# A three-mixer transformer kernel: the triangle inversion starts from a transpose and ends in 64x64 blocks, and the compressed product uses four column groups

## What is computed

```python
def step(state, inp):
    r_t, w_t, k_t, v_t, a_t, b_t = inp
    sa = jnp.einsum('bhvk,bhk->bhv', state, a_t)
    state = (state * w_t[:, :, None, :] + sa[..., None] * b_t[:, :, None, :]
             + v_t[..., None] * k_t[:, :, None, :])
    return state, jnp.einsum('bhvk,bhk->bhv', state, r_t)
```

```python
flat = blocks.transpose(0, 1, 3, 2, 4).reshape(B, nc, G, NSA_CMP_BLOCK * hd)
return jax.nn.gelu(flat @ w1) @ w2
```

## Time and profile before

| | us |
|---|---|
| median of 3 runs | 2197.66 (2193.72 to 2198.87) |
| the profiled execution's own time | 2200.27 |
| its span in the profile | 2198.5 |
| PE busy | 2054.9 (93% of the span) |
| DVE busy, ACT busy | 608.1, 316.1 |
| mean granted TensorE clock | 0.965 of full speed |

### The profile page before, as it was taken

How to read it: one execution, slowest core, us unless ns; L and a number is a source line. 1 busy time by engine, 2 the same in 40 slices (tenths; PEclk the granted TensorE clock), 3 DMA queues, 4 the chain that set the end, 5 groups by cost and what they waited for, 6 DMA issues and landing times.

```text
span 2198.5 us, 24406 instructions
## 1 busy us (share of the span) xinstructions
PE 2054.9 (93%) x9982; PEld 1171.2 (53%) x9982; DVE 608.1 (28%) x1191; ACT 316.1 (14%) x703; POOL 65.0 (3%) x68
## 2 busy tenths in 40 slices
PE   8988999999998999999778999999999999999996
PEld 7766688847766678846634333333333333333332
DVE  0467453312367430004632111111111111111112
ACT  1324110001324210002420000000000000000001
POOL 0022000000022000000010000000000000000000
PEclk9989999999979999999886999999999999999999
DMA  7430078864320045444107999999999999999995
GB/s 296 153 116 1 1 283 303 344 229 171 144 96 31 20 165 228 153 166 153 48 7 290 409 428 429 428 428 429 429 428 428 429 428 429 429 428 427 429 428 252
DMA packets 43823, 599.77 MB, mean 273 GB/s; under 512 B 4992, under 2 KB 5296, under 8 KB 7888
## 3 DMA queue, kind: packets, MB, share of 16 engines
q1 hardware_dynamic: 43760, 598.87, 66.5%
HBM read 597.78 MB, written 1.07 MB: 272 GB/s over the span
## 4 chain that ended last, share of the span: by engine, by line
PE 68%; DMA 22%; DVE 7%; ACT 1%; issue 1%; SPq 0%; DVEq 0%; ACTq 0%
DMA ring<-in_stream 22%; PE ps L1821 14%; PE ps L1234 14%; PE ps L1255 7%; PE ps L376 6%; PE ps L1848 3%; PE ps L390 2%; PE ps L1161 2%; PE ps L1803 2%; PE ps L1898 2%; PE ps L1810 2%; PE ps L1586 1%; PE ps L777 1%; PE ps L789 1%; DVE SB L762 1%
## 5 line engine op out<-in xcount | busy, mean ns | idle before, releaser
L1821 PE MATMUL ps<-ring,HT 128*64 128x512 f32 x2176 | 488.8, 599 | 11.0 <-DMA ring<-in_stream 11.0
L1821 PEld LDWEIGHTS ps<-ring,HT 128*64 128x64 f32 x2176 | 147.9, 137 | 326.5 <-issue 277.1
L1234 PE MATMUL ps<-XT,ring 128*128 128x256 f32 (+1 forms) x1536 | 306.0, 362 | 3.3 <-DVE XT L313 3.3
L1234 PEld LDWEIGHTS ps<-XT,ring 128*128 128x128 f32 x1536 | 271.9, 190 | 36.8 <-DVE XT L313 3.7
L1848 PE MATMUL ps<-ring,HT 128*64 128x512 f32 x1088 | 248.0, 598 | 33.7 <-DMA ring<-in_stream 32.8
L1848 PEld LDWEIGHTS ps<-ring,HT 128*64 128x64 f32 x1088 | 72.6, 136 | 196.1 <-issue 121.3
L1255 PE MATMUL ps<-ring,HT 128*128 128x512 f32 x352 | 151.7, 592 | 0.0
L376 PE MATMUL ps<-XT,ring 128*128 128x256 f32 x576 | 126.6, 383 | 1.3 <-DMA ring<-in_stream 1.3
L1956 DVE TENSOR_SCALAR HT<-ps 128x512 f32<-128x512 f32 x34 | 23.5, 692 | 350.3 <-PE ps L1821 350.3
L376 PEld LDWEIGHTS ps<-XT,ring 128*128 128x128 f32 x576 | 110.7, 192 | 17.0 <-issue 1.7
L1255 PEld LDWEIGHTS ps<-ring,HT 128*128 128x128 f32 x352 | 66.7, 190 | 82.4 <-issue 82.3
(11 more groups left out here) (394 smaller groups left out, 1841.0 us busy)
## 6 DMA issues: line engine op xcount, KB each, us to landing
ring<-in_stream SPq DMA_DIRECT2D x278, 2048.0 KB, 14.6
SB<-in_ln SPq DMA_DIRECT2D x8, 512.0 KB, 9.6
SB<-mod_rows SPq DMA_DIRECT2D x1, 3072.0 KB, 9.8
CST<-in_const SPq DMA_DIRECT2D x1, 1362.0 KB, 5.4
PAR<-in_layer SPq DMA_DIRECT2D x2, 558.5 KB, 11.2
X<-in_x SPq DMA_DIRECT2D x1, 1024.0 KB, 4.9
HN<-in_head_norm SPq DMA_DIRECT2D x2, 512.0 KB, 12.1
SB<-in_gains SPq DMA_DIRECT2D x2, 512.0 KB, 9.8
```

The source lines that it names most:

```text
L1234: m = pe.matmul(ps[:, 2 * (f % 2) + a, j * T + cols.start:j * T + cols.stop], w[:, k, a, j * P:(j + 1) * P], XT[:, k, cols], start=k == 0, ...
L1821: m = pe.matmul(ps[HD * half:HD * (half + 1), a, :], XE[:, 2 * b + k, q * SLOTS_E:(q + 1) * SLOTS_E], w[:, k, a, half, :], start=False, st ...
```

## The change

1. `TM` and `TT` are no longer set to identities. The first level of both halves is done without a product: DVE masks the triangle into `MK` and adds the identity into `TT` (`inverse_first_dve`); PE transposes the eight masked matrices through banks 5 and 6 (`inverse_first_pe`), DVE adds the identity to the transposes and writes `TM` (`inverse_turned_dve`).
2. The last level (half steps 12 and 13) takes only the one 64x64 block per unit that is off the diagonal: four 64x64 products from `MM` itself without a mask, a 64x256 copy on ACT, four 64x64 products for `TT` alone, and one 64x256 copy on DVE in place of two 128x512 adds.
3. The loop starts at half step 2 (h = s+2) and has 18 steps. The attention keeps its lag of two steps, so attention unit u goes with half step u+4, and units 10 and 11 share their steps with the first chunk's parts. The early output projection of t=0 moves from steps 17 and 18 of 20 to steps 16 and 17 of 18.
4. The compressed product's two sums over 16 matmuls become four sums over 8, one in each group of 32 columns of the array (PSUM rows 0 to 127 instead of 0 to 63); the number of matmuls stays 32. DVE adds the two halves (one 64x256 copy more, and an add where a copy was).

```diff
-            L(nc.vector.tensor_copy(SM[:, 32:40], ps[:, 4, 0:8]))
-            v.wait_ge(S("start_loaded"), 32)
-            idb = ident.unsqueeze(1).broadcast_to([P, 8, P])
-            I(nc.vector.tensor_copy(TM, idb))
-            nc.vector.tensor_copy(TT, idb).then_inc(S("rw_init"), 1)
+            nc.vector.tensor_copy(SM[:, 32:40], ps[:, 4, 0:8]).then_inc(S("rw_init"), 1)
...
+        def inverse_done(l, s):
+
+            return 26 * l + (s + 3 if s < 2 else 2 * s + 2 if s < 12 else s + 13)
+
+        def inverse_first_dve(v, l):
+
+            idb = ident.unsqueeze(1).broadcast_to([P, 4, P])
+            v.wait_ge(S("start_loaded"), 32)
+            for s in range(2):
+                us = inverse_half(s)
+                nc.vector.tensor_tensor(MK[:, us, :], MM[:, us, 0, :], inverse_mask(s), ALU.mult).then_inc(S("rw_mk"), 1)
+            for s in range(2):
+                us = inverse_half(s)
+                v.wait_ge(S("rw_mk"), 12 * l + s + 1)
+                nc.vector.tensor_tensor(TT[:, us, :], MK[:, us, :], idb, ALU.add).then_inc(S("rw_tm"), 1)
+
+        def inverse_first_pe(pe, l):
+            pe.wait_ge(S("rw_bk"), l + 1)
+            for s in range(2):
+                pe.wait_ge(S("rw_mk"), 12 * l + s + 1)
+                for i in range(4):
+                    m = pe.transpose(ps[:, 5 + s, i * P:(i + 1) * P], MK[:, 4 * s + i, :], ident)
+                m.then_inc(S("rw_z_ps"), 1)
+
+        def inverse_turned_dve(v, l):
+            idb = ident.unsqueeze(1).broadcast_to([P, 4, P])
+            for s in range(2):
+                v.wait_ge(S("rw_z_ps"), 14 * l + s + 1)
+                nc.vector.tensor_tensor(TM[:, inverse_half(s), :], ps[:, 5 + s, :].rearrange("p (u s) -> p u s", u=4), idb,
+                                        ALU.add).then_inc(S("rw_tm"), 1)
...
+            if s < 4:
+                pool.wait_ge(S("rw_tm"), 26 * l + s - 1)
...
         def inverse_update_dve(v, l, s):
-            us = slice(4 * (s % 2), 4 * (s % 2) + 4)
-            v.wait_ge(S("rw_dt"), 14 * l + s + 1)
-            if s >= 2:
-                v.wait_ge(S("rw_tm"), 28 * l + 2 * s - 2)
+            us = inverse_half(s)
+            v.wait_ge(S("rw_dt"), 12 * l + s - 1)
+            v.wait_ge(S("rw_tm"), inverse_done(l, s - 2))
+            if s >= 12:
+                nc.vector.tensor_copy(TT[0:HD, us, HD:P], ps[0:HD, 7, 0:256].rearrange("p (u s) -> p u s", u=4)
+                                      ).then_inc(S("rw_tm"), 1)
+                return
...
+            pe.wait_ge(S("rw_tm"), inverse_done(l, s - 2))
+            if s > 2:
+                pe.wait_ge(S("rw_zc"), 12 * l + s - 2)
+            if s < 12:
+                pe.wait_ge(S("rw_mk"), 12 * l + s + 1)
             for i in range(4):
                 u = 4 * (s % 2) + i
-                m = pe.matmul(ps[:, 5, i * P:(i + 1) * P], MK[:, u, :], TM[:, u, :], start=True, stop=True)
+                if s < 12:
+                    m = pe.matmul(ps[:, 5, i * P:(i + 1) * P], MK[:, u, :], TM[:, u, :], start=True, stop=True)
+                else:
+                    m = pe.matmul(ps[HD:P, 5, i * HD:(i + 1) * HD], MM[0:HD, u, 0, HD:P], TM[0:HD, u, 0:HD], start=True, stop=True)
...
+            if s == 2:
                 pe.wait_ge(S("cmp_x"), l + 1)
+            if s >= 12:
+                for i in range(4):
+                    u = 4 * (s % 2) + i
+                    m = pe.matmul(ps[0:HD, 7, i * HD:(i + 1) * HD], ZM[HD:P, u, 0:HD], TT[HD:P, u, HD:P], start=True, stop=True)
+                m.then_inc(S("rw_dt"), 1)
+                return
...
-            for j in range(16):
-                for i in range(2):
-                    m = pe.matmul(ps[32 * i:32 * (i + 1), 7, 0:256], N_FL[i][:, j, :], w[i][:, j, :], start=j == 0, stop=j == 15)
+            for j in range(8):
+                for half in range(2):
+                    for i in range(2):
+                        q = 2 * half + i
+                        m = pe.matmul(ps[32 * q:32 * (q + 1), 7, 0:256], N_FL[i][:, 8 * half + j, :], w[i][:, 8 * half + j, :],
+                                      start=j == 0, stop=j == 7, tile_position=(0, 32 * q))
...
-            nc.vector.tensor_copy(x, ps[0:64, 7, 0:256]).then_inc(S("cmp_x"), 1)
+            L(nc.vector.tensor_copy(y, ps[64:128, 7, 0:256]))
+            nc.vector.tensor_tensor(x, y, ps[0:64, 7, 0:256], ALU.add).then_inc(S("cmp_x"), 1)
...
-        HALF_LEVELS, ATT_LAG = 14, 2
-        STEPS = HALF_LEVELS + 6
+        FIRST_HALF, HALF_LEVELS, ATT_LAG = 2, 14, 2
+        STEPS = HALF_LEVELS - FIRST_HALF + 6
...
-            inverse_product_pe(pe, l, 0)
+            inverse_first_pe(pe, l)
+            inverse_product_pe(pe, l, FIRST_HALF)
             for s in range(STEPS):
                 u, at = s - ATT_LAG, NU * l + s - ATT_LAG
-                j, part = divmod(s - HALF_LEVELS, 3)
-                if s + 1 < HALF_LEVELS:
-                    inverse_product_pe(pe, l, s + 1)
+                h = s + FIRST_HALF
+                j, part = divmod(h - HALF_LEVELS, 3)
+                if h + 1 < HALF_LEVELS:
+                    inverse_product_pe(pe, l, h + 1)
                 if unit_scores(u):
                     attention_scores_pe(pe, at)
-                if s < HALF_LEVELS:
-                    inverse_update_pe(pe, l, s)
+                if h < HALF_LEVELS:
+                    inverse_update_pe(pe, l, h)
...
-                if s in (STEPS - 3, STEPS - 2):
-                    mix_early_pe(pe, l, 0, s - (STEPS - 3))
+                if s in (STEPS - 2, STEPS - 1):
+                    mix_early_pe(pe, l, 0, s - (STEPS - 2))
...
-            inverse_level_dve(v, l, 0)
-            inverse_level_dve(v, l, 1)
+            inverse_first_dve(v, l)
             gla_mask_dve(v, l)
+            inverse_turned_dve(v, l)
             cmp_hidden_dve(v, l, L)
```

More of the change, by code:

```diff
@@ L739, in rwkv_mask_dve, with inverse_half, inverse_mask @@
                                     ALU.mult).then_inc(S("rw_mm"), 1)
-        def inverse_level_dve(v, l, s):
-            n, us = s // 2, slice(4 * (s % 2), 4 * (s % 2) + 4)
-            lev = cst("levels")[:, n * P:(n + 1) * P].unsqueeze(1).broadcast_to([P, 4, P])
-            nc.vector.tensor_tensor(MK[:, us, :], MM[:, us, 0, :], lev, ALU.mult).then_inc(S("rw_mk"), 1)
+        def inverse_half(s):
+            return slice(4 * (s % 2), 4 * (s % 2) + 4)
+        def inverse_mask(s):
+            return cst("levels")[:, (s // 2) * P:(s // 2 + 1) * P].unsqueeze(1).broadcast_to([P, 4, P])
@@ L756, in inverse_update_dve @@
+            nc.gpsimd.tensor_tensor(MK[:, us, :], MM[:, us, 0, :], inverse_mask(s), ALU.mult).then_inc(S("rw_mk"), 1)
         def inverse_update_dve(v, l, s):
-            us = slice(4 * (s % 2), 4 * (s % 2) + 4)
-            v.wait_ge(S("rw_dt"), 14 * l + s + 1)
-            if s >= 2:
-                v.wait_ge(S("rw_tm"), 28 * l + 2 * s - 2)
+            us = inverse_half(s)
+            v.wait_ge(S("rw_dt"), 12 * l + s - 1)
[4 more added lines that the diff above has]
+                return
@@ L796, in inverse_product_act @@
             act.wait_ge(S("rw_z_ps"), 14 * l + s + 1)
-            if s >= 2:
-                act.wait_ge(S("rw_dt"), 14 * l + s - 1)
-            g = 4 * (s % 2)
-            nc.scalar.activation(ZM[:, g:g + 4, :].rearrange("p u s -> p (u s)"), ps[:, 5, :], ACT.Copy).then_inc(S("rw_zc"), 1)
+            if s >= 4:
+                act.wait_ge(S("rw_dt"), 12 * l + s - 3)
+            us = inverse_half(s)
+            if s < 12:
+                to, src = ZM[:, us, :].rearrange("p u s -> p (u s)"), ps[:, 5, :]
+            else:
+                to, src = ZM[HD:P, us, 0:HD], ps[HD:P, 5, 0:256].rearrange("p (u s) -> p u s", u=4)
+            nc.scalar.activation(to, src, ACT.Copy).then_inc(S("rw_zc"), 1)
         def chunk_removed_pe(pe, l, j):
             if j == 0:
-                pe.wait_ge(S("rw_tm"), 28 * (l + 1))
+                pe.wait_ge(S("rw_tm"), 26 * (l + 1))
+                pe.wait_ge(S("rw_init"), l + 1)
             else:
@@ L2069, in mixers_act @@
                     rwkv_bk_act(act, l)
-            inverse_product_act(act, l, 0)
+            inverse_product_act(act, l, FIRST_HALF)
             cmp_act(act, l)
@@ L2073, in mixers_act @@
                 u, at = s - ATT_LAG, NU * l + s - ATT_LAG
-                if s + 1 < HALF_LEVELS:
-                    inverse_product_act(act, l, s + 1)
+                if s + FIRST_HALF + 1 < HALF_LEVELS:
+                    inverse_product_act(act, l, s + FIRST_HALF + 1)
                 if s == 0:
@@ L2111, in mixers_dve @@
                     attention_scores_dve(v, at, I, L)
-                if s < HALF_LEVELS:
-                    inverse_update_dve(v, l, s)
+                if h < HALF_LEVELS:
+                    inverse_update_dve(v, l, h)
                 elif part == 0:
@@ L2149, in _ @@
                 cmp_pool(pool, l)
-                for s in range(2, HALF_LEVELS):
```

(1 more changed line is left out.)

19 lines of the change are left out of this document (3 added, 16 removed).

## The result

The changed kernel takes 2191.7 us (median of 8 runs) against 2197.5 of the kernel before; the ratio is 0.9969, with a 95% interval of 0.9955 to 0.9982. One of the eight took 2681.5 us at a mean granted clock of 0.731; the other seven took 2187.6 to 2195.5 us, and the ratio goes by them. The profiled execution took 2195.54 us with a span of 2193.7, 4.8 less than the span of before.

The account below looks back on a forecast made before the run. PE bounds the kernel, with 68% of the chain that ended last. Full clock would gain 25.6 us in both tails; a clock fall there leaves 3.6, giving 2194 against the median 2197.66, range 2177 to 2200 for 8 in 10.

Parts of the forecast that it names:

- Compressed product: Stage's head on PE: four column groups cut 8.95 us to some 5.1, 3.5 saved per layer.
- rival 4: Compressed product's four groups don't run side by side: 3 us slower in all, 2201; chance 0.08 of the forecast's 0.56.
- Start of the inversion: After the compressed product: 2.2 of 3.5 us spent on transposes and waits; adds 1.3 us earlier, 1.0 kept.
- Small products: Last doubling: 0.35 us each for the 64x64 product and update, 0.43 for DVE's copy; step 9 saves 0.7.
- Waits in steps 11 to 13: PE waits for the attention's way through DVE and ACT in these steps: 1.9 us.
- The new wait: Ahead of the output projection, PE waits for the merge's copy behind the second solve's copy: 1.95 us.
- The tail at full clock: Step 10 to the turn back: at full clock it ends at 255.2, gaining 12.8 us per layer, 25.6 in both.
- The clock: Falls in the tail: near 226.6 in one layer (4.3 us gained), near 219.8 in the other (nothing); 3.6 in all.
- 1 (the clock stays up): Clock stays at 1.0 in the tail: 25.6 us gained, 2172; chance 0.14.
- 2 (late fall, one layer only): Clock falls behind the first chunk or in one layer only: 7 to 15 us gained, about 2187; chance 0.22.
- 3 (slower): Clock falls with the first small products at 216.4 and rises late: 6.8 us lost in both layers, 2204.5; chance 0.08.

Follow-up runs that it names:

- four added products and the merge first: Changed kernel with DVE's copy of the attention's result before the second solve's copy, plus one unread 128x128 by 128x256 product in each of steps 10 to 13: 2173.3 us.
- merge first: Changed kernel with DVE's copy of the attention's result put ahead of the second solve's copy at step 16: 2177.6 us median; its second profiled run 2170.3.
- the inversion alone: Changed kernel with the compressed product back on two column groups, so only the inversion's change remains: 2198.6 us, ratio 1.0006 against the kernel before.
- the small products: Changed kernel with three unread 64x64 products added in each of steps 10 to 16, 21 per layer: 2198.1 us, ratio 0.9997 against the kernel before.
- the four groups alone: Kernel before with only the compressed product's four column groups and DVE's copy and add, inversion as it was: 2190.2 us, ratio 0.9967.
- twelve products in the pairs: Changed kernel, attention's copy first, four large products in steps 10 to 13, plus twelve per layer ahead of GLA's scores of pieces 2 to 7: 2173.9 us.
- seven large: Changed kernel with one unread 128x128 by 128x256 product added in each of steps 10 to 16: 2180.8 us, ratio 0.9929 against the kernel before.

## Why the prediction was right or wrong

The number was near (2194 against 2191.7, and faster by 0.3% where "no change" had the larger chance), but that is luck in part, since two errors cancel in the sum: the stages gained 4.3 us more than I had, and outside them, where I had nothing, 3.95 were lost (0.65 and 3.30) and 0.89 gained.

- **Compressed product**: forecast 5.1 us and 3.5 saved; measured 4.95 and 5.29 in the two layers. Four groups work side by side (rival 4 is out). Alone they gave 6.8 us for both layers together; this is the term that the result is made of.
- **Start of the inversion**: the waits came as listed (POOL's mask 1.21, ACT's copy 0.73), and in layer 1 the adds were 1.39 us early (19.49 before, 18.10 after), forecast 1.3. In layer 0 a slow piece of the clock at 151.0 to 154.4 left 0.16. (The 10.7 us that the prediction reads between the two points before is 10.6 by its own rows; nothing rests on it.)
- **Small products**: I took 0.35 us for four; four 64x64 products took 0.60 (216.10 to 216.70), an update 0.61 (217.25 to 217.86). I had read four rows, which are two products, as four, and their weights have 128 rows and not 64. Step 9 took 4.68 us (211.42 to 216.10) in place of 5.22 (211.38 to 216.60), so 0.54 saved, not 0.7.
- **Waits in steps 11 to 13**: forecast 1.9 us, measured nearly none. The two errors partly cancel: what the blocks take more, some 0.25 us for each product or update, the attention's chain no longer has to wait for.
- **The new wait**: forecast 1.95, measured 1.71 in both layers.
- **The tail at full clock**: forecast a turn back at 255.2, 12.8 us per layer gained. The kernel with four added products and the merge first, in which the clock held, has 255.05, where the added work (some 2 us) and the wait that is gone (1.4) nearly cancel. The nearer test is the stage of 111.72 in layer 1 of the second profile of merge first, with no added work and the full clock: with the wait of 1.4 us back it would be 113.1 (an estimate), 14.0 less than before. So the work was priced right to about a microsecond.
- **The clock**: forecast a fall near 226.6 in one layer (turn back at 263.7) and a fall near 219.8 with no gain in the other. Measured 226.1 and 264.61, and in layer 1 the same case: 82 us behind the start of the compressed product in place of 85. So the stages gained 7.9 us in the profile where I had 3.6. Where in a tail the clock falls isn't fixed by the program (37.6 or 3.4 slow us in one and the same), so a forecast of the place to within a microsecond was luck; that it falls there in this kernel is borne out by the clock of 0.955 to 0.959 in all seven runs.
- **What failed** is a step that I left out: the sum ended at the turn back, and I took the rest to shift as it is. The slow stretches between the layers didn't shift with it: 3.30 us went there in the profiled execution (how firmly that hangs on the change, see the last section).
- **Rivals**: 1 (the clock stays up) is refuted for this kernel; it is what one gets once larger products stand in steps 10 to 13, or in the lucky executions with the merge first. 2 (late fall, one layer only) wasn't seen in the profile of the changed kernel; the inversion alone had it in layer 1. 3 (slower) wasn't seen.

## What to carry to other kernels

Before small work is made smaller, look at the granted clock in the windows around it: where PE is the bound and the clock sits near its fall, taking away full-size products can lower the clock for all that follows, and a few useless large products may buy more than they cost (here seven per layer gave 10.9 us, and four per layer, some 2 us of PE time, gave 18.4 together with the merge put first). It pays only where the clock is then really held: in the pairs' stretch twelve products gave 2.6 us in the layer where it held and cost 3.35 in the one where it didn't. Judge it by the mean granted clock of many runs, not by one profile. And where a copy and the work of a chain meet on one engine, put first the one that the next large block waits for.

## What the runs showed of the hardware

- The clock fell from 1.0 to 0.5 with hardly a gap on PE ahead of it: busy 3.40 of 3.40 us before, 2.85 of 2.90 after (223.2 to 226.1), 3.90 of 3.90 with the small products. It held with PE busy 22.96 of 27.20 us when large products were among the work.
- Executions of one program differ in where it falls: 3.4 or 37.6 us of slow tail, 2170 or 2188 us in all. A profile shows one of them; the one of the four groups alone was its fastest run, 5.5 us under its median.
- Even the code ahead of the stage, the same in all kernels, doesn't bring it to one time: the first scores of GLA (L472) start at 114.1 to 114.2 us in six profiles and at 115.8 to 116.4 in eight. The six have at most 3.4 slow us in the tail of layer 0; of the eight, all but the one with twelve products in the pairs have 6.8 to 23.9. The two profiles of merge first are one of each kind (114.20 and 116.17), and so are those with seven large and with 21 small products. Two profiles alone therefore don't show what an edit does to the clock there; the clocks of all runs do. Why the arrival and the clock go together stays open.
- The stretch from the turn back of layer 0 to the compressed product of layer 1, which is the same code in all kernels but the last, took 374.5 to 376.6 us in seven profiles and 378.0 to 378.1 in six. These six have a slow piece between 573 and 592 us that the others lack. Summed up, the slow pieces that begin between 573 us and the compressed product come to 23.9 us in the three shortest (374.5 to 375.2), 27.3 in the next four and 30.7 in the six, and half of that difference is nearly the whole spread. The same kernel, merge first, had 375.75 in one profile and 378.06 in the other. So the 3.30 us between the layers need not be the change's doing; what decides it stays open.
- 32-column weights in four groups: 64 records in 3.66 us at full clock, 0.057 each, against 0.204 of a full-width record with as many columns. A quarter of that would be 0.051: the four groups ran side by side at 3.6 times the rate of one full-width record after another.
- Four 64x64 fp32 products with 64 columns take 0.60 us, against 1.06 for four of 128x128 with 128 columns: an eighth of the arithmetic for over half of the time.
